# When weight sums are copied and added, and when a retention head's rows are turned, in a decoder layer on one core

## The reference

```
n    = rms_norm(x, norm1_g)
proj = n @ w_in            # q_att, c_kv, q_idx, k_idx, w_idx, r_q, r_k, r_v, r_gate, g_att, g_ret
att  = top-256 sparse attention, 8 heads of 128, over shared k and v
ret  = chunkwise retention, 4 heads, chunks of 128; group norm per head
y_att = att @ w_att_branch
y_ret = (silu(r_gate) * ret) @ w_ret_branch
h    = x + (sigmoid(g_att) * y_att + sigmoid(g_ret) * y_ret) @ w_out
out  = h + top-2 of 16 experts (one of 4 groups first) on rms_norm(h, norm2_g)
```

## Time and profile before

| what | value |
|---|---|
| median of 3 runs | 1546.06 us |
| profiled execution, its own time | 1538.81 us |
| span of that execution, first to last instruction | 1536.7 us |
| TensorE busy (6518 matmuls) | 1392.8 us, 91% |
| VectorE busy | 1101.8 us, 72% |
| ScalarE busy | 871.6 us, 57% |
| GpSimd busy | 674.0 us, 44% |
| mean granted TensorE clock | 0.948 |
| DMA moved | 336.76 MB, mean 219 GB/s |

### The profile page before, as it was taken

The page is one execution under the profiler, slowest core; times in us unless marked ns, Lnnn a source line. Parts: engine busy times, 40 slices in busy tenths (PEclk is TensorE's granted clock), DMA queues, the critical chain, the costliest instruction groups (busy, mean ns, idle before and its releaser), DMA issues.

```text
span 1536.7 us, 19629 instructions
## 1 busy us (share of the span) xinstructions
PE 1392.8 (91%) x6518; PEld 1140.7 (74%) x6518; DVE 1101.8 (72%) x1581; ACT 871.6 (57%) x1528; POOL 674.0 (44%) x474
## 2 busy tenths in 40 slices
PE   6998699999998949587998999999999499999995
PEld 6877588878877837455765888888787388888884
DVE  6828699899999813365751527798933789999994
ACT  5247444345843826475762546454334478888884
POOL 4621245554453713322201545555332457765654
PEclk9997899999999979699999999999999599999998
DMA  5997968895754687989914547665155799989995
GB/s 197 361 223 141 218 212 310 210 304 178 274 179 166 215 305 239 212 245 241 196 40 171 190 122 227 217 221 188 55 202 192 252 314 248 268 230 363 267 296 76
DMA packets 153364, 336.76 MB, mean 219 GB/s; under 512 B 14896, under 2 KB 32688, under 8 KB 149040
## 3 DMA queue, kind: packets, MB, share of 16 engines
q1 hardware_dynamic: 111904, 227.49, 43.7%
q0 software_dynamic: 28496, 82.85, 25.2%
q10 hardware_dynamic: 12864, 25.17, 4.4%
HBM read 323.92 MB, written 125.83 MB: 293 GB/s over the span
## 4 chain that ended last, share of the span: by engine, by line
PE 62%; DMA 13%; DVE 10%; issue 5%; POOL 4%; ACT 4%; SPq 1%; ACTq 0%; DVEq 0%; POOLq 0%
PE ps L975 17%; PE ps L977 17%; PE ps L976 17%; DMA sums_dram<-in_w_in 3%; PE ps L1296 3%; DMA sums_dram<-sums_dram 3%; DVE hits L2146 2%; PE ps L1430 2%; PE ps L1286 1%; POOL w_lo L2628 1%; DMA t_raw<-turned_dram 1%; DMA e_raw<-in_w_up 1%; DMA w_raw<-in_w_in 1%; DVE n_lo L2036 1%; DMA ret_dram<-rT_out 1%
## 5 line engine op out<-in xcount | busy, mean ns | idle before, releaser
L2628 POOL TENSOR_TENSOR w_lo<-w_raw,w_hi 128x512 fp32r<-128x512 f32 (+1 forms) x264 | 383.0, 1465 | 484.4 <-ACT w_hi L1502 483.6
L1502 ACT CAST w_hi<-w_raw 128x512 fp32r<-128x512 f32 (+1 forms) x264 | 161.4, 616 | 326.0 <-PE ps L977 259.8
L975 PE MATMUL ps<-n_hi,w_hi 128*128 128x512 f32 x624 | 247.6, 397 | 24.4 <-POOL w_lo L2628 22.6
L977 PE MATMUL ps<-n_hi,w_lo 128*128 128x512 f32 x624 | 245.4, 393 | 0.0
L976 PE MATMUL ps<-n_lo,w_hi 128*128 128x512 f32 x624 | 245.4, 393 | 0.0
L2566 DVE TENSOR_TENSOR e_lo<-e_raw,e_hi 128x2048 fp32r<-128x2048 f32 x93 | 213.0, 2293 | 23.2 <-ACT e_hi L1942 23.1
L975 PE MATMUL ps<-w_hi,n_hi 128*128 128x512 f32 (+1 forms) x528 | 202.8, 384 | 10.1 <-DVE n_lo L2036 5.3
L976 PE MATMUL ps<-w_lo,n_hi 128*128 128x512 f32 (+1 forms) x528 | 201.6, 382 | 0.0
L977 PE MATMUL ps<-w_hi,n_lo 128*128 128x512 f32 (+1 forms) x528 | 201.3, 381 | 0.0
L1942 ACT CAST e_hi<-e_raw 128x2048 fp32r<-128x2048 f32 x93 | 177.7, 1914 | 34.1 <-DMA e_raw<-in_w_up 17.4
L2784 POOL DMA_INDIRECT out<-e_y,dest x62 | 139.5, 2250 | 98.8 <-DMA out<-e_y,dest 69.5
(11 more groups left out here) (287 smaller groups left out, 2657.1 us busy)
## 6 DMA issues: line engine op xcount, KB each, us to landing
w_raw<-sums_dram SPq DMA_DIRECT2D x128, 256.0 KB, 3.5
e_raw<-in_w_gate SPq DMA_DIRECT2D x64, 512.0 KB
e_raw<-in_w_up SPq DMA_DIRECT2D x64, 512.0 KB
e_raw<-in_w_down SPq DMA_DIRECT2D x32, 1024.0 KB
w_raw<-in_w_in SPq DMA_DIRECT2D x80, 256.0 KB, 4.3
sums_dram<-in_w_in POOLq DMA_DIRECT2D x20, 1024.0 KB, 14.8
sums_dram<-in_w_in SPq DMA_DIRECT2D x16, 1024.0 KB, 8.9
sums_dram<-sums_dram POOLq DMA_DIRECT2D x16, 1024.0 KB, 8.3
```

The lines of the kernel that those rows point to most:

```text
L975: mm(out, a[0], b[0], start=first, stop=False, skip_group_check=skip)
L977: return mm(out, a[1], b[0], start=False, stop=last, skip_group_check=skip)
L1502: nc.scalar.copy(w_hi[c % NH][:, :width], split_from(c)[:, :width]).then_inc(hi_ready, 1)
L2628: G.tensor_tensor(w_lo[c % NH][:, :width], split_from(c)[:, :width], w_hi[c % NH][:, :width].bitcast(F32), ALU.subtract).then_inc(lo_ready, 1)
```

## The change

Four things, with the code below.

1. In retention, `turn(h)` comes after the half product that it stood before, on TensorE, ScalarE and in the order of banks. The turns of heads 2 and 3 stand together at the end.
2. Group 2's three stages are issued in the projection loop after chunks 2, 8 and 14.
3. Groups 4 to 7 are copied and added one at a time: group 4 copied after q row tile 1 is scaled and added at tiles 2 to 4; group 5 copied at tile 5, added at tiles 6 and 7; group 6 copied and added after tile 7's rows; group 7 copied after the fifth low part of product m6's block and added in the same place of m7, m4 and m5. SyncE waits for group 5 at tile 5 instead of tile 3 (then loading four chunks of m6 instead of three), for group 6 eight chunks before the branches and for group 7 at the middle of the branch chunks.
4. The high parts of the first chunks of m6 are cast at tile 7 instead of 5. The buffer `qT_lo0` moves from the fourth `w_raw` buffer to the place of `w_up`, which `first_out0` uses too, so VectorE waits for the stores of `first_out` before q tile 2.

```diff
-            [(wr_at + 4 * BANK * (NR - 1), wr_at + 4 * BANK * (NR + NH - 1)),
+            [(up_at, wr_at + 4 * BANK * (NR + NH - 1)),
...
-        SUMS_GATES, SUMS_BRANCH = 512, 768
+        SUMS_GATES, SUMS_BRANCH = 512, (640, 768)
...
-            ("phase2", 1), ("phase1", 2), ("turn", 0), ("first", 1), ("phase2", 2), ("phase1", 3), ("turn", 1), ("first", 2),
-            ("turn", 2), ("phase2", 3), ("first", 3), ("turn", 3)]
+            ("phase2", 1), ("phase1", 2), ("first", 1), ("turn", 0), ("phase2", 2), ("phase1", 3), ("first", 2),
+            ("turn", 1), ("phase2", 3), ("first", 3), ("turn", 2), ("turn", 3)]
...
-                if t == 3:
+                if t == 5:
                     sp.wait_ge(sums_added, SUMS_GATES)
-                    for c in range(m6, m6 + NR - 1):
+                    for c in range(m6, m6 + NR):
                         load_chunk(c)
...
+                if c == branch_at + NQ // 2:
+                    sp.wait_ge(sums_added, SUMS_BRANCH[1])
...
-                    sp.wait_ge(sums_added, SUMS_BRANCH)
+                    sp.wait_ge(sums_added, SUMS_BRANCH[0])
...
-                if i == 3:
-                    out_turn(2)
-                    out_phase2(3)
+                if i >= 2:
+                    out_turn(i - 2)
+                if i:
+                    out_phase2(i)
                 if i in (1, 2):
-                    out_phase2(i)
                     out_phase1(i + 1)
                 hi(c)
                 out_stats(i)
-                if i in (1, 2):
-                    out_turn(i - 1)
...
             out_qT(0, 1)
+            out_turn(2)
             out_turn(3)
...
-                    if m == 5 * HA:
+                    if m == 7 * HA:
...
+                if (t, g) == (2, 0):
+                    dve.wait_ge(first_stored[0], 16 * 8)
...
-                done = 64 * groups[0] if groups[0] < 4 else 128 * groups[0] - 128
+                done = 64 * groups[0] if groups[0] < 4 else 128 * groups[0] - 192
...
-            for stage in range(3):
-                add_sums(stage, (2,))
...
-            adds_at = {36: (0, (3,)), 44: (1, (3,)), 52: (2, (3,))}
+            adds_at = {2: (0, (2,)), 8: (1, (2,)), 14: (2, (2,)), 36: (0, (3,)), 44: (1, (3,)), 52: (2, (3,))}
...
-                if i == 0:
-                    copy_sums((4, 5))
                 if i == 2:
                     scale_rows(0)
-                if i >= 2:
-                    add_sums(i - 2, (4, 5))
             scale_rows(1)
+            copy_sums((4,))
             for t in range(2, NT):
                 scale_rows(t)
-                if t == 2:
-                    add_sums(2, (4, 5))
-                if t == 4:
-                    copy_sums((6, 7))
-                if t >= 6:
-                    add_sums(t - 6, (6, 7))
+                if t < 5:
+                    add_sums(t - 2, (4,))
+                elif t == 5:
+                    copy_sums((5,))
+                elif t == 6:
+                    add_sums(0, (5,))
+                    add_sums(1, (5,))
+            add_sums(2, (5,))
+            copy_sums((6,))
+            for stage in range(3):
+                add_sums(stage, (6,))
             for c in range(m6, m6 + NH - 1):
                 lo(c)
-            add_sums(2, (6, 7))
...
             for b in blocks[m6 // KT:number["wo1b"]]:
-                ahead(b[0])
+                for k in range(KT):
+                    lo(number[b[0]] * KT + k + NH - 1)
+                    if k == 4 and b[0] in REST[:4]:
+                        stage = REST.index(b[0])
+                        if stage == 0:
+                            copy_sums((7,))
+                        else:
+                            add_sums(stage - 1, (7,))
```

More of the change, by code:

```diff
@@ L861, in _ @@
                     bk.wait_read(sp, ("lg", HA * (NT - 1) - 1))
-                    for c in range(m6 + NR - 1, m6 + NR + NH - 1):
+                    for c in range(m6 + NR, m6 + NR + NH - 1):
                         load_chunk(c)
```

## The result

The changed kernel takes 1512.3 us (median of 4 runs, 1511.5 to 1513.2) against 1546.2 for the kernel before: ratio 0.9773, 95% interval 0.9751 to 0.9796, 33.9 us less. I had said 1502 and 43.7 us less.

The account below looks back on a forecast made before the run. TensorE, busy 91% of a 1536.7 us span, was taken as the bound, so only filled holes count. Gains 11.7 + 24.1 + 13.2 - 5.3 = 43.7 us off the 1546.1 median gave 1502, range 1485 to 1520.

Parts of the forecast that it names:

- rivals A and C: A: group 7's copies hold SyncE's queue, 1519, chance 0.17; C: retention stays bound by its own loads, 1512, chance 0.11.
- Part 1: Projection: group 2's sums issued inside the loop remove TensorE's idle before the fourth weight chunk, +11.7 us.
- I take -1.0: Projection loop: cost of group 2's stages lying beside chunk loads, -1.0 us, bounds 0 and -6.
- rival E: Whole kernel: the queue re-makes the holes elsewhere and only the projection gain is left, 1534 us, chance 0.05.
- Part 2: Retention: copies of groups 4 and 5 leave and turns come after the next half product, +24.1 us, bounds +13.4 and +34.6.
- 3.5 for the stores: Start of attention: VectorE's wait for the last store of turned rows goes, +3.5 us, bounds 0 and 3.5.
- none over 6 as a sign of being right: Retention: no ScalarE wait over 6 us for a weight chunk between 520 and 580 us would show the forecast right.
- The landing, taken at 11.3: End of retention: head 3's copy waits for head 2's stores to land before reusing the buffers, 11.3 us lost.
- Attention, +9.7: Attention: no q row is scaled late behind a held GpSimd issue, so VectorE's idle goes, 9.7 us, bounds 5 and 10.
- Part 4: Products: group 7's copies beside SyncE's loads delay a weight chunk and leave TensorE idle, -5.3 us.
- The bound of -22.4: Products: worst case for group 7's copies, the load queue held as in the earlier retention hole, -22.4 us.
- The gap at the start of the products: Products: a gap at their start longer than the earlier 4.4 us would show the forecast wrong.

Follow-up runs that it names:

- g2_small: Changed kernel with group 2's four accumulating DMAs cut to 32 of their 512 rows, every instruction kept (sums wrong): ratio 0.9823 to the kernel before.
- g7_in_attention: Changed kernel with group 7's four copies moved from the products to the end of attention, its adds left in the products: ratio 0.9758 to the kernel before.

## Why the prediction was right, and where its terms failed

The time fell in the range, outside the band of my own forecast (1496 to 1509) and at the level that I had given to rivals A and C, by neither mechanism. What was right is the main step: copies and sums leave the retention and are spread over attention, and these two stretches gave 24.9 and 9.1 us. That 1512 lies as near to 1502 as it does is in part luck, as the last point says. By the steps:

- **Part 1, +11.7, measured under 3: the step that failed.** The hole went, as said. "What is late next: the low part ... ready near 165" was right too. What failed is "I take -1.0", the cost of the stages beside the chunk loads, read off group 3, with a bound of -6. It is 6 to 7 us (g2_small), at the bound or beyond it. Group 3's stages stand at chunks 36 to 52; at 2 to 14 and at 14 to 26 the same transfers re-made the gap in pieces. The hole itself was taken at 11.8 from one execution, 8.5 to 8.8 in two others. This is what I had given 0.05 as rival E, the hole re-made elsewhere, come true in one stage. I had set it aside on the strength of the window of 760 to 800 us, which says nothing of the window at 160, where loads landed in 7.3 us instead of 2.7 beside the stages. The Trainium skill, DMA: Bandwidth & Descriptors, section "Issuing engines are not separate DMA queues", says that DMAs of all engines run on the same 16 and interleave; the trace agrees. Why group 3's stages cost so little stays open: from 280 to 320 us of the kernel before the DMA share is 0.99 and chunks of n land in 10.4 us (median), yet TensorE is full.

```profile
280.00:320.00 40.00, 40.00 (x178) 33.11 (x178) 34.16 (x72) 14.98 (x27) 21.32 (x17) 1.00 0.99 276
```

- **Part 2, +24.1, and 3.5 for the stores: 24.9 measured.** One wait of 7.02 us before a cast stood between 520 and 580 us (at 542.66); I had added 4.2 and had named none over 6 as a sign of being right, so that sign was missed. The landing, taken at 11.3, was 8.3 and 1.9. The gain is that of the copies that left (32 us, by subtraction). The order costs 6.3; my terms for it (-1.0, -3.5, -11.3, and +4.5 for the gap filled) came to -11.3, so the sign was in them, and I did not say that the reorder by itself loses.
- **Attention, +9.7: 9.1.** One issue was held, 7.9 us at the third copy of group 5, and no q row came late by it, as said: TensorE's wait of 6.9 us for a q row near 708 us, behind the 27.2 us hold of the kernel before, is gone. No run changed this part by itself. SyncE's wait for the sums at tile 5 was 1.6 us and covered.
- **Part 4, -5.3: -10.0.** (By its own terms, 16.7 less 11, the sum should read -5.7.) The bound of -22.4 held, the mechanism was not the one at work: a gap of about the size and in the place that I had named, made by something else. The gap at the start of the products, 4.7 us against 4.4, was a sign of being wrong that came true, if narrowly. I had looked for a held SyncE, and wrote that "the issues themselves delay a low part by 2.6 us, within its slack". The issue on GpSimd was held 7.8 us, the case of the earlier trace rows, which I had priced in attention and not here. The gap is 6.3 us, and TensorE then worked 9.5 us at a granted clock of 0.80 (820 to 830), 1.9 us lost by my estimate. These 8.2 us are about what g7_in_attention won back.
- **The sum and the median.** The gain of the traces, 27.3 us, and that of the medians, 33.9, differ by the 7 us by which the first trace was better than its median. Two errors of size, -9 and -5, were in part hidden by that. On the trace's scale the forecast was 16.4 us too good.

## What to carry to other kernels

A DMA issue on an engine that also computes is priced by what stands behind it in that engine's queue: where a trace shows one held issue, expect one wherever a similar burst comes, and put bursts where nothing urgent follows (here the end of attention, 7 to 9 us). Moving transfers off the critical path into a phase with loads of its own can move the hole there. The share of a calm window says nothing of it, and the share alone did not tell here either (0.99 with TensorE full, 0.98 with gaps): cut the bytes of the moved transfers, as g2_small does, and look. A gap taken from one execution wants a second one before it enters a sum.

## What the runs showed of the hardware

**Held issues of GpSimd.** They last until what this queue has in flight has landed: 7.8 us with one 1 MB copy in flight, 15.4 with three, 6.1 with one and less other traffic. In the changed kernel the held issue ended at 817.24 us, and the copy ahead of it had landed at 817.05; in g2_small the times are 819.47 and, for the last of three, 819.27. Their place follows the transfers issued before: it was the second copy of group 7 in the changed kernel and in g7_in_attention, the fourth when group 2's transfers were small, and an accumulating DMA when the copies went through ScalarE. What count decides the place was not settled.

**VectorE beside GpSimd.** VectorE's instruction on six columns took 0.17 us alone and 5.72 us at 189.78, beside four low parts on GpSimd; it ended within 0.03 us of them (195.50, 195.47). The 31 of this line took 12.8 us in the kernel before and 21.4 in the changed one. In g2_small, where TensorE's gaps went, VectorE was just as busy. What the longer instructions cost was not measured apart.

```profile
189.78 5.72 DVE L2164 TENSOR_SCALAR top_change<-top_count 128x6 int32<-128x6 f32 x1
...
190.21 5.26 POOL L2631 TENSOR_TENSOR w_lo<-w_raw,w_hi 128x512 fp32r<-128x512 f32 x4
```
